# First expert's slot lists and gathers: from the end of the routing part to behind the barrier

## The reference

```python
logits = xt @ w_router + b_router                  # xt: the normed rows, 1024 x 1024
top_logit, top_idx = lax.top_k(logits, 4)          # 4 of 32 experts for each token
gates = jax.nn.softmax(top_logit)
gu = lax.ragged_dot(xs, w_gate_up, group_sizes) + b_gate_up[e_sorted]
act = (lin + 1.0) * (gate * sigmoid(1.702 * gate)) # both clamped at 7
out = lax.ragged_dot(act, w_down, group_sizes) + b_down[e_sorted]
y = sum over the 4 chosen experts of gate * out    # added to x, then a last RMSNorm
```

## Time and profile before

| | |
|---|---|
| median of 3 runs | 2567.62 us (2565.17 to 2568.31) |
| span of the profiled execution | 2566.9 us |
| TensorE busy | 2471.5 us, 96% |
| VectorE busy | 1506.3 us, 59% |
| ScalarE busy | 1226.7 us, 48% |
| GpSimd busy | 329.9 us, 13% |
| moved by DMA | 536.68 MB, 209 GB/s over the span |

### The profile page before, as it was taken

How to read it: one execution, slowest core, us unless ns; L and a number is a source line. 1 busy time by engine, 2 the same in 40 slices (tenths; PEclk the granted TensorE clock), 3 DMA queues, 4 the chain that set the end, 5 groups by cost and what they waited for, 6 DMA issues and landing times.

```text
span 2566.9 us, 41888 instructions
## 1 busy us (share of the span) xinstructions
PE 2471.5 (96%) x14427; PEld 1980.3 (77%) x14428; DVE 1506.3 (59%) x1486; ACT 1226.7 (48%) x1246; POOL 329.9 (13%) x379
## 2 busy tenths in 40 slices
PE   8999999999999989976999999999999999999996
PEld 7987777998888878974788777777777886778775
DVE  4312333332333235355789876888876997688877
ACT  6413444220112021064577665666655775667665
POOL 0000000000000000042121212121121221212110
PEclk9999999999999999997999999999999999999998
DMA  4133243224332212447789987898977997899988
GB/s 129 34 50 54 66 73 80 49 50 49 50 50 81 99 66 91 146 167 263 257 317 384 371 296 257 319 381 287 369 252 258 376 381 271 306 335 331 387 278 304
DMA packets 262285, 536.68 MB, mean 209 GB/s; under 512 B 28952, under 2 KB 79896, under 8 KB 261120
## 3 DMA queue, kind: packets, MB, share of 16 engines
q1 hardware_dynamic: 241184, 488.96, 57.3%
q0 software_dynamic: 21024, 46.65, 6.7%
HBM read 492.92 MB, written 42.63 MB: 209 GB/s over the span
## 4 chain that ended last, share of the span: by engine, by line
PE 51%; DMA 1%; DVE 1%; issue 0%; ACT 0%; POOL 0%; ACTq 0%; POOLq 0%; DVEq 0%
PE m_y L2158 5%; PE m_gate L2158 5%; PE m_gate L2162 4%; PE m_lin L2158 4%; PE m_gate L2160 4%; PE m_lin L2162 4%; PE m_lin L2160 4%; PE m_y L2160 4%; PE m_y L2162 4%; PE m_spill L2200 4%; PE m_turn L2212 2%; PE m_turn L2150 1%; PE m_gate L2168 1%; PE m_y L2168 1%; PE m_spill L2196 1%; PE m_lin L2168 1%
## 5 line engine op out<-in xcount | busy, mean ns | idle before, releaser
L1973 DVE TENSOR_TENSOR m_w_lo<-raw,m_w_hi 128x2048 fp32r<-128x2048 f32 x384 | 874.6, 2288 | 253.7 <-ACT m_w_hi L1847 234.8
L1847 ACT CAST m_w_hi<-raw 128x2048 fp32r<-128x2048 f32 x384 | 733.3, 1911 | 446.2 <-PE m_lin L2162 230.1
L106 PE MATMUL c_bank<-h_hi_r,ring_hi 128*128 128x512 f32 x640 | 251.7, 393 | 0.9 <-PEq L396 0.9
L108 PE MATMUL c_bank<-h_lo_r,ring_hi 128*128 128x512 f32 x640 | 249.5, 390 | 0.0
L109 PE MATMUL c_bank<-h_hi_r,ring_raw_r 128*128 128x512 f32 x640 | 249.2, 389 | 0.0
L147 ACT CAST ring_hi<-ring_raw 128x2048 fp32r<-128x2048 f32 x43 | 82.1, 1908 | 280.4 <-DMA ring_raw<-in_w_in 128.3
L2158 PE MATMUL m_gate<-m_w_hi,m_x_hi 128*128 128x512 f32 x512 | 209.6, 409 | 0.0
L2158 PE MATMUL m_y<-m_w_hi,m_a_hi 128*128 128x512 f32 x512 | 206.1, 403 | 1.5 <-DVE m_a_lo L2025 1.5
L2162 PE MATMUL m_gate<-m_w_hi,m_x_lo 128*128 128x512 f32 x512 | 201.1, 393 | 0.0
L2160 PE MATMUL m_y<-m_w_lo,m_a_hi 128*128 128x512 f32 x512 | 201.0, 393 | 0.0
L2158 PE MATMUL m_lin<-m_w_hi,m_x_hi 128*128 128x512 f32 x512 | 200.7, 392 | 0.0
(11 more groups left out here) (336 smaller groups left out, 4539.9 us busy)
## 6 DMA issues: line engine op xcount, KB each, us to landing
raw<-in_w_gate_up SPq DMA_DIRECT2D x512, 512.0 KB
raw<-in_w_down SPq DMA_DIRECT2D x256, 512.0 KB, 12.3
ring_raw<-in_w_in SPq DMA_DIRECT2D x31, 1024.0 KB, 9.4
gates<-work POOLq DMA_DIRECT2D x32, 256.0 KB, 2.6
work<-gates SPq DMA_DIRECT2D x8, 1024.0 KB, 7.2
v<-in_x SPq DMA_DIRECT2D x8, 512.0 KB, 12.5
ring_raw<-in_w_branch_b SPq DMA_DIRECT2D x4, 1024.0 KB, 5.3
ring_raw<-in_w_branch_a SPq DMA_DIRECT2D x4, 1024.0 KB, 5.2
```

The lines of the kernel that those rows point to most:

```text
L106: pe.matmul(out, left_hi(k), right_hi(k), start=first and k == kts[0], stop=False, skip_group_check=True)
L108: pe.matmul(out, left_hi(k), right_lo(k), start=False, stop=False, skip_group_check=True)
L1847: act.copy(w_hi[:, p % WS].rearrange("p k b n -> p (k b n)"), raw[:, raw_slot(m)].rearrange("p k b n -> p (k b n)")).then_inc(signals.whi, 1)
L1973: dve.tensor_tensor(w_lo[:, p % WS].rearrange("p k b n -> p (k b n)"), raw[:, raw_slot(m)].rearrange("p k b n -> p (k b n)"), f32(w_hi[:, ...
```

## The change

The lists and gathers of the first expert leave the routing part. In the experts' part GpSimd issues them first: the list of 128, a wait for it, the gather of `xg`, then the four spill lists, a wait, and the gather of `xs_g`. `rows_in` is raised when `xg` has landed, no longer when both have. ScalarE and VectorE split the weight panels 0 and 1 before x, where they split panel 0 alone. TensorE waits for `first_spill` and runs `xs_turn` after the products of panel 0, where it ran it right behind `x_turn(0)`. Expert 1's list still comes after the waits for both gathers.

```diff
@@ output_and_route, GpSimd
             pool.wait_ge(sent, 16 * TT * TOP_K)
-            pool.dma_start(slot_in[:, 0, :], slot_rows[0:P, 0:2]).then_inc(signals.in_listed[0], 16)
-            for quarter in range(NG):
-                pool.dma_start(slot_in[SPILL * quarter:SPILL * (quarter + 1), 1, :],
-                               slot_rows[P:P + SPILL, 2 + 2 * quarter:4 + 2 * quarter]).then_inc(spill_listed, 16)
             for s in range(HT):
                 pool.wait_ge(stored[s], 16 * len(range(s, TT, HT)))
             pool.wait_ge(finished, 16 * (TT + 2))
-            pool.wait_ge(signals.in_listed[0], 16)
-            pool.indirect_dma_start(out=xg[:, :], out_offset=None, in_=h_rows[:, :],
-                                    in_offset=bass.IndirectOffsetOnAxis(ap=slot_in[:, 0, 0:1], axis=0)) \
-                .then_inc(signals.gathered[0], 16)
-            pool.wait_ge(spill_listed, 16 * NG)
-            pool.indirect_dma_start(out=xs_g[:, :], out_offset=None, in_=h_rows.rearrange("r (g c) -> (r g) c", g=NG),
-                                    in_offset=bass.IndirectOffsetOnAxis(ap=slot_in[:, 1, 0:1], axis=0)) \
-                .then_inc(signals.first_spill, 16)
@@ experts, GpSimd
+            pool.dma_start(slot_in[:, 0, :], slot_rows[0:P, 0:2]).then_inc(signals.in_listed[0], 16)
+            pool.wait_ge(signals.in_listed[0], 16)
+            pool.indirect_dma_start(out=xg[:, :], out_offset=None, in_=h_rows[:, :],
+                                    in_offset=bass.IndirectOffsetOnAxis(ap=slot_in[:, 0, 0:1], axis=0)) \
+                .then_inc(signals.gathered[0], 16)
+            for g in range(NG):
+                pool.dma_start(slot_in[SPILL * g:SPILL * (g + 1), 1, :],
+                               slot_rows[P:P + SPILL, 2 + 2 * g:4 + 2 * g]).then_inc(spill_listed, 16)
+            pool.wait_ge(spill_listed, 16 * NG)
+            pool.indirect_dma_start(out=xs_g[:, :], out_offset=None, in_=h_quarters,
+                                    in_offset=bass.IndirectOffsetOnAxis(ap=slot_in[:, 1, 0:1], axis=0)) \
+                .then_inc(signals.first_spill, 16)
             pool.wait_ge(signals.gathered[0], 16)
+            pool.sem_inc(signals.rows_in, 1)
             pool.wait_ge(signals.first_spill, 16)
-            pool.sem_inc(signals.rows_in, 1)
@@ experts, ScalarE (VectorE likewise, with its own counts)
-            split(0, 6, 0)
+            for m in range(2):
+                split(m, m + 6, 0)
             for r in range(2):
                 x_split(r, 0)
-            for m in range(1, 4):
+            for m in range(2, 4):
                 split(m, m + 6, 0)
@@ experts, TensorE
             x_turn(0)
             first_second = about(pe, held, 0)[0]
-            xs_turn(first_second)
             pe.wait_ge(signals.picked_gu, OPEN + 1)
             pe.wait_ge(signals.xlo, OPEN + 2)
             for m in range(4):
                 pe.wait_ge(signals.wlo, OPEN + m + 1)
                 gate_up(m, m + 6)
+                if m == 0:
+                    pe.wait_ge(signals.first_spill, 16)
+                    xs_turn(first_second)
```

More of the change, by code:

```diff
@@ L1129, in output_and_route @@
         slotted, sent = sem("slotted"), sem("sent")
-        spill_listed = sem("spill_listed")
         stored, finished = [sem(f"stored{s}") for s in range(HT)], sem("finished")
@@ L1626, in experts @@
         old_rows, old_spill = end("old_rows"), end("old_spill")
+        spill_listed = end("spill_listed")
         block = ctx.enter_context(nc.Block())
@@ L2111, in _ @@
             pick_expert(0, 0, signals.picked_gu)
-            split(0, 6, OPEN + 1)
+            for m in range(2):
+                split(m, m + 6, OPEN + m + 1)
             for r in range(2):
                 x_split(r, 0)
-            for m in range(1, 4):
+            for m in range(2, 4):
                 split(m, m + 6, OPEN + m + 1)
```

## The result

The changed kernel took 2572.01 us (median of 16 runs, 2567.85 to 2576.18), the kernel before 2566.18 us on the same chip (16 runs, 2561.91 to 2568.31): 1.0022 of it, with a 95% interval of 1.0015 to 1.0029. That is 5.8 us slower, just past the 0.2% that can be told from none (the interval reaches to both sides of it). The forecast was 2570.9 us and a loss of 3.3 us; the time lies inside its range. The profiled execution took 2572.49 us.

What follows compares the result with a forecast made beforehand. TensorE was taken to bound it, busy throughout the expert loop, so delays at its start reach the end one for one. 2.7 (xg) + 0 (spill wait) + 0.6 (spill transposes) = 3.3 us on 2567.62: 2570.9 us, range 2565.8 to 2574.8.

Steps and rivals of the forecast that it cites:

- Barrier: End of the routing part: GpSimd's DRAIN takes 2.84 us instead of 5.46, and the barrier opens 7.4 us earlier.
- Rival C: The DRAIN at the block's end stays at 5.46 us; all behind it 2.6 us later, 2573.5 us; chance 0.10.
- The list: First list, behind the barrier in a filling panel stream: lands 2.7 us after issue, between 1.8 and 5.5.
- The gather: Gather of xg in the panel stream: 8.7 us, bounds 4.4 and 9.6; rows transposed 5.3 us later than before.
- The signal: Release of TensorE's first transposes: rows of xg land at 1179.7, transposes start at 1179.8.
- Transposes to first product: With the first weight splits done before x arrives: 3.4 us instead of 6.0; first product 2.7 us later than before.
- Spill rows: Gather of xs_g lands before panel 0 ends, hidden by 0.6 us; its transposes and branch cost 0.6 us.
- Rival D: The spill rows come late and TensorE stands 2.5 us behind panel 0: 2573.4 us; chance 0.12.
- Expert 1: Rows of expert 1 ready at 1208.6, TensorE transposes them at 1212.2: hidden by 3.6 us, no wait.
- TensorE's clock: Start of the experts: low level until 5.7 us after the first product, as before; bounds 2.7 us less or more.
- Rival B: The young panel stream doesn't delay list (1.8 us) or gather (4.4): first product 2.5 us earlier, 2566.1 us; chance 0.20.
- the 2.0 us that I had put on the two splits: VectorE's two weight splits beside the gather of xg hold off GpSimd's descriptor work, up to 2.0 us.

Runs made afterwards that it cites:

- the second profile of before: The kernel before, unchanged, run and profiled again as a control: 2565.01 us, 0.9999 of the kernel before.
- the second profile: The changed kernel, unchanged, run and profiled again as a control: 2571.03 us, 1.0021 of the kernel before.
- one experiment: Against the changed kernel: list and gather of xg kept in the routing part, rows_in raised before the spill lists, one weight split before x; 2571.77 us, 1.0022 of before.
- the short hold: The changed kernel with SyncE's loads of panels 4 to 11 held only until the first list has landed: 2571.25 us, 1.0018 of before.

## Why the prediction was right and where it was short

The forecast was right in kind and its size was short: 3.3 us of loss were forecast, 5.8 measured. That the time itself came within 1.1 us is in part luck, since the forecast stood on a median of three runs, 2567.62 us, where sixteen gave 2566.18. "Slower by over 0.2%" had a chance of 0.21 and is, just, what the ratio of 1.0022 says.

Right in kind: the gain at the barrier was more than eaten by a list and a gather in the panel stream (holding the stream gave the whole loss back), and the chain behind the rows was shortened as worked out. Term by term, behind T:

- *Barrier.* Predicted T + 8.3 by a DRAIN of 2.84 us; measured 7.6 and 2.67; most of the 0.7 us is that the last scatter landed 0.7 us sooner behind T, which the second profile of before has too. Rival C, a fixed long DRAIN, falls; its length goes with the DMAs in flight (5.46, 5.21, 5.45 and 5.92 us in four profiles with gathers before it, 2.67 to 3.09 where they are behind it).
- *From the barrier to the list's issue.* Predicted 1.5, measured 1.8.
- *The list.* Predicted 2.7 us, "nearer to the idle row", since the stream was only filling; measured 5.0, and 6.4 in the second profile. This is the term that was mis-sized. The row I argued from was right (57 GB/s in the microsecond of the issue, 227 in the next), but not what it meant: the list's first packets moved only in 1168.5 to 1169, 3.5 us after the issue. They met not the stream of the moment of issue, but the one some microseconds on.
- *List to gather.* Predicted 0.8, measured 0.3.
- *The gather.* Predicted 8.7, measured 8.1 (7.2 in the second profile); of these, 1.77 us are its own work, where I had said 2 to 3.
- *The signal.* Predicted at the landing. Measured 0.9 us later, since the sender stands on GpSimd's queue behind the wait for the spill lists; I had put this wait down for the spill rows alone. It is the wait that the forecast missed, and the moved signal bears it out (0.1 us from landing to transposes).
- *Transposes to first product.* Predicted 3.4, measured 3.4.
- *Spill rows.* Predicted hidden by 0.6 us; they landed at T + 29.8 and were asked for at T + 32.7, hidden by 3.0. Their gather was predicted at T + 23.7 and issued at 24.0, but took 5.8 us instead of 7.3, and panel 0 ended 1.1 us later than predicted. Their transposes cost 0.2, not 0.6: at the end of panel 0 TensorE already had its high clock. Rival D falls for this kernel and is real where the spill rows start later, as one experiment shows.
- *Expert 1.* No wait, as predicted.
- *TensorE's clock.* Predicted at the low level until 5.7 us after the first product; a granted clock of 0.74 over 1185 to 1190 puts the rise 4.8 us after it, an estimated gain of 0.4 us. The second fall, at the first m_turn, the prediction did not have; it cost 1.7 us in this profile.

Together the first product was predicted at T + 25.5 and came at T + 27.2: 1.7 us more, of which the list has 2.3 and the signal 0.9, against gains of 0.7 at the barrier and 0.6 in the gather. The sum was made against a profile of before whose seam was 1.2 us longer than in its repetition; against that one, the loss is 5.6 us, and 5.8 is timed. Rival B, the young stream that does not hinder, falls: neither list nor gather came near its idle length. The wait of the gather's own work on VectorE's subtractions was real and cost at most 0.8 us here, by estimate (1.77 against 1.00 us), and nothing in the second profile, where the gather came behind both. By the Trainium skill, "SBUF — State Buffer" (SBUF: two separate sides), a VectorE op with two SBUF inputs can hold off a GpSimd op that reads SBUF for its whole length. The trace agrees for the subtraction that is under way when the gather comes (own work 2.54 to 2.68 us against 1.00), not for one that starts during the own work; so the 2.0 us that I had put on the two splits were too much. One sum of the prediction is off: rival B's own terms give 2566.3 or 2565.7 us, not 2566.1, so that the range's lower end, 2565.8, is not under both. Nothing hangs on it here.

Left open: what keeps the first packets of a GpSimd gather back for 3.3 us from the end of its own work once SyncE's panels are in the queues, where it is 0.7 without them; and why the rows took 5.0 us from the first packet to the landing in the one profile with the short hold. One other question wasn't tried: whether a gather whose first packets move before the panels are issued, so that they need not wait for its landing, goes undelayed.

## What to carry to other kernels

A small dependent DMA that is moved behind a barrier can lose its quiet place, as here: what opens first there is the bulk load of the next part, and a chain of two such DMAs (a list, then a gather by it) pays the delay twice. Issue the chain's first link before the barrier, hold the bulk load until the second has landed, and send the signal right behind the landing that it stands for, ahead of any wait for something else on the same queue. And compare seams from an event that both kernels share, with a second profile of each: here two profiles of one program differed by 1.2 us at the first product, where the effect looked for was 4.4 to 5.6.

## What the runs showed of the hardware

- In SyncE's stream of panels a GpSimd gather moved its first packet 3.2 to 3.4 us after the end of GpSimd's own work on it, without the stream 0.6 to 0.7 us after, and it was the same whether the panels had been issued 6.1 or 0.3 us ahead. From issue to landing: list 1.8 to 2.0 against 5.0 to 6.4 us; gather 4.2 to 5.9 against 7.2 to 11.0.
- A gather's own work on GpSimd took 1.00 to 1.02 us alone. Issued during one of VectorE's subtractions (two SBUF inputs, 2.29 us), it lasted until that one's end and 0.9 us more (1.4 to 3.0 us in all). The four plain spill lists took 2.07 us beside a subtraction too, as without one.
- The DRAIN at the end of GpSimd's block ended 1.4 to 1.7 us after the last gather's landing, where one was in flight, and took 2.67 to 3.09 us where all gathers were behind it, a landing list included.
- A pause of 2.35 us on TensorE, ahead of the first m_turn, was followed by 3.4 us at the low clock in 10 of the 13 profiles; of the two profiles of the kernel before, one has it and the other not.
